# Layer norms at the end of a projection: last two output tiles by token halves, the root's guess in PSUM, and the second half's sums inside the next stage's loop

## What is computed

```python
for layer in range(2):
    if layer == 0: mix = concat(s5_mixer(...), stick_breaking(...)) @ w_out_ab
    else:          mix = hgrn2_mixer(...) @ w_out_c
    h = layer_norm(ALPHA * h + mix, ln_mix_g[layer], ln_mix_b[layer])
    hid = square(relu(h @ mlp_w_up[layer] + mlp_b_up[layer]))
    h = layer_norm(ALPHA * h + hid @ mlp_w_down[layer] + mlp_b_down[layer], ln_mlp_g[layer], ln_mlp_b[layer])
return h[:, N_META:, :]
```

## Time and profile before

| | |
|---|---|
| median of 3 runs | 1380.58 us (1379.8 to 1380.92) |
| the profiled execution | 1380.39 us, its span 1378.5 us |
| granted TensorE clock, mean | 0.987 |
| PE busy | 1323.0 us, 96% of the span |
| DVE, ACT, POOL busy | 45%, 37%, 38% |
| chain that ended last, by engine | PE 83%, DVE 6%, ACT 6% |

### The profile page before, as it was taken

How to read it: one execution, slowest core, us unless ns; L and a number is a source line. 1 busy time by engine, 2 the same in 40 slices (tenths; PEclk the granted TensorE clock), 3 DMA queues, 4 the chain that set the end, 5 groups by cost and what they waited for, 6 DMA issues and landing times.

```text
span 1378.5 us, 21807 instructions
## 1 busy us (share of the span) xinstructions
PE 1323.0 (96%) x9502; PEld 1185.7 (86%) x9502; DVE 624.2 (45%) x1048; ACT 512.8 (37%) x734; POOL 530.4 (38%) x224
## 2 busy tenths in 40 slices
PE   6999998999999999999999999998999999999996
PEld 5998855999999999999998988876798888888885
DVE  6899544456530024412456456464556300344125
ACT  4334487435222222221365335263362222223124
POOL 1001153355443344454554123145654444444450
PEclk9999999999999999999999999999999999999998
DMA  6211200121333322333211111112212333323321
GB/s 181 92 62 33 63 1 0 62 92 62 93 92 92 93 92 92 92 93 92 92 62 62 62 62 62 61 63 91 92 62 92 92 94 107 105 92 92 92 62 61
DMA packets 141791, 108.27 MB, mean 79 GB/s; under 512 B 8096, under 2 KB 139376, under 8 KB 141696
## 3 DMA queue, kind: packets, MB, share of 16 engines
q1 hardware_dynamic: 141296, 106.77, 25.6%
q10 hardware_dynamic: 400, 0.11, 0.0%
HBM read 104.77 MB, written 2.10 MB: 78 GB/s over the span
## 4 chain that ended last, share of the span: by engine, by line
PE 83%; DVE 6%; ACT 6%; issue 2%; POOL 1%; DMA 1%; DVEq 0%; SPq 0%; ACTq 0%
PE pb L709 62%; PE pb L875 2%; PE pb L721 2%; PE pb L876 2%; PE pb L877 2%; PE pb L1076 1%; PE pb L815 1%; PE pb L816 1%; ACT wh L1292 1%; PE pb L753 1%; PE pb L814 1%; PE pb L1074 1%; DVE bc L2276 1%; DVE st L2315 1%; PE pb L985 1%
## 5 line engine op out<-in xcount | busy, mean ns | idle before, releaser
L565 POOL TENSOR_TENSOR wl<-raw,wh 128x2048 fp32r<-128x2048 f32 x85 | 396.6, 4666 | 531.1 <-ACT wh L1292 531.1
L709 PE MATMUL pb<-hh,wh 128*128 128x264 f32 (+1 forms) x1160 | 302.0, 318 | 1.8 <-DVE tmp L2098 1.2
L709 PE MATMUL pb<-hh,wl 128*128 128x264 f32 (+1 forms) x1160 | 297.5, 314 | 0.0
L709 PE MATMUL pb<-hl,wh 128*128 128x264 f32 (+1 forms) x1160 | 297.3, 314 | 0.0
L1292 ACT ACTIVATE wh<-raw 128x2048 fp32r<-128x2048 f32 x97 | 185.0, 1908 | 96.7 <-DMA raw<-in_mlp_w_down 63.2
L709 PEld LDWEIGHTS pb<-hh,wh 128*128 128x128 f32 x1160 | 191.2, 189 | 17.6 <-issue 3.7
L709 PEld LDWEIGHTS pb<-hl,wh 128*128 128x128 f32 x1160 | 191.2, 189 | 13.9 <-issue 1.2
L709 PEld LDWEIGHTS pb<-hh,wl 128*128 128x128 f32 x1160 | 191.1, 189 | 13.5
L709 PE MATMUL pb<-hidh,wh 128*128 128x264 f32 (+1 forms) x720 | 191.9, 321 | 0.0
L709 PE MATMUL pb<-hidh,wl 128*128 128x264 f32 (+1 forms) x720 | 191.1, 320 | 0.0
L709 PE MATMUL pb<-hidl,wh 128*128 128x264 f32 (+1 forms) x720 | 190.3, 318 | 0.0
(11 more groups left out here) (391 smaller groups left out, 2055.3 us busy)
## 6 DMA issues: line engine op xcount, KB each, us to landing
raw<-in_mlp_w_up SPq DMA_DIRECT2D x32, 1024.0 KB, 5.3
raw<-in_mlp_w_down SPq DMA_DIRECT2D x32, 1024.0 KB, 5.5
raw<-in_w_in_c SPq DMA_DIRECT2D x16, 1024.0 KB, 5.3
raw<-in_w_in_ab SPq DMA_DIRECT2D x8, 1024.0 KB, 5.6
raw<-in_w_out_ab SPq DMA_DIRECT2D x4, 1024.0 KB, 5.0
raw<-in_w_out_c SPq DMA_DIRECT2D x4, 1024.0 KB, 4.9
x_tok<-in_x SPq DMA_DIRECT2D x2, 1024.0 KB, 8.0
raw<-in_s_w_glu SPq DMA_DIRECT2D x1, 1024.0 KB, 5.4
```

Source lines behind the costliest of these rows:

```text
L565: pool.tensor_tensor(wl[:, c % RING, :], raw[:, c % RING, :], wh[:, c % RING, :].bitcast(F32), ALU.subtract).then_inc(w_lo, 1)
L709: mm = pe.matmul(pb[:, bank + b, 0:z_ - a], lhs, rhs[:, a:z_], start=first and hi and k == 0, stop=last and k == len(todo) - 1)
```

## The change

`TWO` is true for norms 0 and 2. The counts that semaphores are compared with get helper tables (`DS`, `SQ`, `SC`, `CT` in place of `n`, `6 * n`, `9 * n`, `13 * n`), since norms 0 and 2 now count one more each.

1. Norms 0 and 2: tiles 6 and 7 both run by token halves, in the order tile 6 a = 0, tile 7 a = 0, tile 6 a = 1, tile 7 a = 1. The four sums of the first half go into the products of tile 6 a = 1. DVE's addition of tile 6, its total, ACT's square and POOL's addition of that square become two halves each. The second ones follow later: on DVE after the first `scale_`, on ACT ahead of `last_square(1)`, on POOL after the first `hl`.
2. All norms: the second half's `first_sum` and `first_squares` leave the end of the stage. They are issued in `run_after` after step 1's and step 3's hh products; `last_square(1)` goes from step 2 to step 3. In norm 3 they go between the transposes of blocks 0 and 1.
3. All norms: ACT writes its guess into PSUM (`ln_part(name, 4, a)`), and DVE's three operations are rewritten so that each reads at most `total` or `tmq` from SBUF beside it.

```diff
+TWO = (True, False, True, False)
+DS = [n + sum(TWO[:n]) for n in range(4)]
...
@@ POOL, lows_ln @@
+                def add_half(a):
+                    pool.wait_ge(squared, SC[n] + (9 if a else 7))
+                    pool.wait_ge(sq_added, SQ[n] + 5)
+                    s_ = part(name, sqs[:, :], a)
+                    pool.tensor_tensor(s_, s_, part(name, squares(6), a), ALU.add).then_inc(sq_added, 1)
...
-                    if t >= 4:
+                    if t == 6 and TWO[n]:
+                        add_half(0)
+                    elif t >= 4:
                         add(t)
...
+                            if a == 0 and m == 0 and TWO[n]:
+                                add_half(1)
@@ PE, last_tile @@
-                first_sum(name, n, 1)
-                first_squares(name, n, 1)
+            def last_tiles(name, n, rh, rl, c, w0, order):
+                kcs = len(order)
+                for a in range(2):
+                    for t in (6, 7):
+                        if a == 0 and t == 7:
+                            pe.wait_ge(*free_bank(name, 7))
+                        for i, kc in enumerate(order):
+                            mm = products_half(name, t, c, w0(kc, t), rh[:, kc, :], rl[:, kc, :], a, i == 0, i == kcs - 1)
+                            if i == kcs - 1:
+                                mm.then_inc(tile_done if a else half_done, 1)
+                            if a and t == 6 and i == 2:
+                                first_sum(name, n, 0)
+                                last_sum(name, n, 0)
+                            if a and t == 6 and i == 4:
+                                first_squares(name, n, 0)
+                            if a and t == 6 and i == 6:
+                                last_square(name, n, 0)
@@ PE, run_after @@
-                pe.wait_ge(*free_bank(tiles[0][0], 0))
+                if not TWO[n]:
+                    pe.wait_ge(*free_bank(tiles[0][0], 0))
...
                         if a == 0 and step == 1:
+                            first_sum(LN_STAGE[n], n, 1)
                             last_sum(LN_STAGE[n], n, 1)
-                        if a == 0 and step == 2:
+                        if a == 0 and step == 3:
+                            first_squares(LN_STAGE[n], n, 1)
                             last_square(LN_STAGE[n], n, 1)
@@ PE, transposes behind norm 3 @@
                     if a == 0 and kc == 0:
+                        first_sum("down11", 3, 1)
                         last_sum("down11", 3, 1)
                     if a == 0 and kc == 1:
+                        first_squares("down11", 3, 1)
                         last_square("down11", 3, 1)
@@ ACT, run_ln @@
                 def guess(a):
-                    guess_inv_sqrt(part(name, total[:, :], a), part(name, tmq[:, 0, :], a), var_out, 2 * n + 1 + a)
+                    act.wait_ge(var_out, 2 * n + 1 + a)
+                    o = part(name, tmq[:, 0, :], a)
+                    me.step(act.activation(o, part(name, total[:, :], a), ACT.Ln))
+                    me.settle()
+                    act.activation(ln_part(name, 4, a), o, ACT.Exp, scale=-0.5).then_inc(guessed, 1)
...
                         if a == 0 and m == 1:
+                            if TWO[n]:
+                                square_half(1)
                             last_square(1)
@@ DVE, layer_norm @@
-                add(6)
-                TT(tot, tops, hm(6), ALU.add).then_inc(d_summed, 1)
+                if TWO[n]:
+                    add_half(0)
+                    dve.wait_ge(centred, CT[n] + 11)
+                    me.settle()
+                    total_half(0)
+                else:
+                    add(6)
+                    TT(tot, tops, hm(6), ALU.add).then_inc(d_summed, 1)
...
                 def root(a):
-                    inv_sqrt(part(name, tmq[:, 0, :], a), part(name, total[:, :], a), part(name, tmq[:, 1, :], a),
-                             ln_part(name, 4, a), 2 * n + 1 + a + (8 if n >= 2 else 0))
+                    o, t = ln_part(name, 4, a), part(name, tmq[:, 1, :], a)
+                    dve.wait_ge(guessed, 2 * n + 1 + a + (8 if n >= 2 else 0))
+                    step(TT(t, part(name, total[:, :], a), o, ALU.mult))
+                    step(STT(t, t, -0.5, o, ALU.mult, ALU.mult))
+                    step(STT(o, t, 1.5, o, ALU.add, ALU.mult))
...
                     scale_(m, 0)
+                    if m == 0 and TWO[n]:
+                        add_half(1)
                     if m == 0:
                         last_add(1)
+                    if m == 0 and TWO[n]:
+                        total_half(1)
```

More of the change, by code:

```diff
@@ L64 @@
          2: [("up10", 0), ("up10", 1), ("up10", 2), ("up10", 3)]}
+TWO = (True, False, True, False)
+DS = [n + sum(TWO[:n]) for n in range(4)]
+SQ = [6 * n + sum(TWO[:n]) for n in range(4)]
+SC = [9 * n + sum(TWO[:n]) for n in range(4)]
+CT = [13 * n + sum(TWO[:n]) for n in range(4)]
 AHEAD = {"up00": 2, "f0": 1, "q0": 1, "up10": 2}
@@ L735, in run @@
                             pe.wait_ge(*free_bank(name, t))
+                        if norm is not None and TWO[norm] and t == KC - 2:
+                            last_tiles(name, norm, rh, rl, s0 + j, lambda kc, t: kc * cols_ + (t % 2) * P, order or range(kcs))
+                            return
                         if norm is not None and t == KC - 1:
@@ L1580, in square, with square_half @@
                 def square(m):
-                    act.wait_ge(centred, 13 * n + (m + 1 if m < 4 else m + 5))
+                    act.wait_ge(centred, CT[n] + (m + 1 if m < 4 else m + 5))
                     if m >= 2:
-                        act.wait_ge(sq_added, 6 * n + m - 2)
+                        act.wait_ge(sq_added, SQ[n] + m - 2)
                     act.activation(flat(name, squares(m)), flat(name, h[:, m, :]), ACT.Square).then_inc(squared, 1)
+                def square_half(a):
+                    act.wait_ge(centred, CT[n] + (13 if a else 11))
+                    act.wait_ge(sq_added, SQ[n] + 4)
+                    act.activation(part(name, squares(6), a), part(name, h[:, 6, :], a), ACT.Square).then_inc(squared, 1)
                 def last_square(a):
-                    act.wait_ge(centred, 13 * n + 12 + a)
-                    act.wait_ge(sq_added, 6 * n + 5)
+                    act.wait_ge(centred, CT[n] + 12 + (a + TWO[n] if a else 0))
+                    act.wait_ge(sq_added, SQ[n] + 5)
                     act.activation(part(name, tmq[:, 1, :], a), part(name, h[:, 7, :], a), ACT.Square).then_inc(squared, 1)
@@ L1601, in run_ln @@
                             square(m)
-                    if t >= 4:
+                    if t == 6 and TWO[n]:
+                        square_half(0)
+                    elif t >= 4:
                         square(t)
@@ L2166, in layer_norm, with add_half, total_half @@
                 step(TT(tops, tops, hm(5), ALU.add))
-                add(6)
-                TT(tot, tops, hm(6), ALU.add).then_inc(d_summed, 1)
+                def add_half(a):
+                    if a:
+                        dve.wait_ge(tile_done, t0 + 7)
+                    else:
+                        dve.wait_ge(half_done, DS[n] + 1)
+                    h6 = part(name, h[:, 6, :], a)
+                    TT(h6, h6, pb[:, a, 0:width(name)], ALU.add).then_inc(centred, 1)
+                def total_half(a):
+                    TT(part(name, total[:, :], a), ln_part(name, 6, a), part(name, h[:, 6, :], a),
+                       ALU.add).then_inc(d_summed, 1)
                 def last_add(a):
-                    dve.wait_ge(tile_done if a else half_done, t0 + KC if a else n + 1)
+                    if a:
+                        dve.wait_ge(tile_done, t0 + KC)
+                    else:
+                        dve.wait_ge(half_done, DS[n] + 1 + TWO[n])
                     h7 = part(name, h[:, 7, :], a)
@@ L2198, in layer_norm @@
                 last_add(0)
-                dve.wait_ge(squared, 9 * n + 7)
+                dve.wait_ge(squared, SC[n] + 7)
                 dve.wait_ge(s1_squared, 2 * n + 1)
```

25 lines of the change are left out of this document (13 added, 12 removed).

## The result

After took 1380.19 us (median of 20 runs, 1376.32 to 1384.24); before, run beside it, 1375.14 us (median of 20, 1374.17 to 1380.92). The ratio of the two is **1.0027, 95% interval 1.0016 to 1.0038**: after is slower, by 3.7 us (2.2 to 5.2). The ratio is that of the means (1380.42 and 1376.65); the medians lie 5.1 us apart, because that of before falls into the shorter of its two groups of executions. The forecast was 1382.6 us and +2.0 us. Two things in the forecast caused this: the level that it started from, and the clock at norm 0.

The account below looks back on a forecast made before the run. Each seam was taken to hang on the second half's last square; its shifts of +0.13, +1.46, +0.40 and 0 us at norms 0 to 3 made +2.0, giving 1382.6 us against the median, range 1380.4 to 1385.0.

Parts of the forecast that it names:

- What bounds the seam: From one product stage to the next, the first pass's last `hl` group trails the second half's last square by 9.4-9.6 us.
- Q: The second half's last square at each norm; the time from the old stage's end to it sets the cost there.
- 1, the earlier start: Norms 0 and 2: token halves bring the first half's variance 1.45 and 0.88 us sooner, partly held by POOL's copy.
- 2, the root: DVE's first root step takes 0.42 us, saving 0.19, 1.92 and 0.83 us in norms 0, 1 and 2.
- 3, from the first scaling to Q: Norms 0 and 2: this path takes 8.63 us, where it was 6.86 and 6.52; called the term that decides.
- Norm 1: Tiles kept; step 1 starts 0.87 us sooner, but the second half's last square comes at 688.40, 1.46 us later.
- Norm 3: Last square moves by one sum, from 1360.23 to about 1360.67; effect on the time 0 (0 to 0.1).
- The sum: Last square after less before: norm 0 +0.13, norm 1 +1.46, norm 2 +0.40, norm 3 0; together +2.0 us.
- the first rival: PE's clock falls again behind norm 0, 2 or both, or before lost it less often: +1.4 to +3.4 us; chance 0.30.
- The base: Time of before that the forecast started from: profiled execution 1380.39 us, 0.19 below the median of the runs.
- The rival for faster: The second pass follows the first `hh`, so each earlier start counts: 4.2 us less, 1376.4; chance 0.07.
- The third rival: DVE's root goes on waiting for POOL's copy: 1.9 us more, 1384.5; chance 0.06.

Follow-up runs that it names:

- run 6: Before with part 3 of the change alone (guess in PSUM), plus `high` moved from behind block 5 to block 7 and POOL's quarter copies later: 1365.01 us, ratio 0.9926.
- run 7: After with `high` moved from behind block 5 to behind block 7 and POOL's quarter copies moved later: 1371.4 us, ratio 0.9975.
- run 11: After with the second half's squares back at step 2, and `high` and POOL's quarter copies moved later: 1370.1 us, ratio 0.9951.
- run 5: After with the second half's first_squares and last_square back from step 3 to step 2: 1376.43 us, ratio 1.0002.
- run 2: Before with part 3 of the change alone (guess in PSUM, DVE's three operations rewritten): 1372.53 us, ratio 0.9972.
- run 4: After with the old root (guess in SBUF, guess * guess first): one execution, 1384.9 us.
- run 10: After with small useless products in both of PE's waits in norms 0 and 2 (4 ahead of step 0, 5 behind it): 1378.57 us, ratio 1.001.
- run 9: After, unchanged, run once more for more executions and a second trace: 1379.36 us, ratio 1.0022.
- run 8: Before with small useless products (8 at norm 0, 11 at norm 2) in PE's wait for the first `hh`: 1371.33 us, ratio 0.9977.

## Why the prediction was right or wrong, point by point

- **What bounds the seam**: right. The last hl group followed Q by 9.4 to 9.6 us in every kernel that kept the queue, and by 7 to 8.1 us where `high` was moved (runs 6, 7, 11). One step less before Q was one step less of seam, three times (run 5).
- **1, the earlier start**: right. From the addition of tile 5, the first half's variance was forecast at 10.55 and 10.45 us and came at 10.65 and 10.53; the wait for POOL's copy is there, smaller (0.18 us in norm 0, and 0.42 in norm 2 for 0.8).
- **2, the root**: the step is 0.43 at once, as forecast. The Trainium skill, "SBUF — State Buffer", section "Who interferes with whom", says that a VectorE instruction with at most one SBUF input, outside its two-port modes, doesn't contend with GpSimd, and that one with two SBUF inputs contends with a GpSimd instruction that reads SBUF; the traces agree (0.43 us beside POOL's copy in after and run 2; 1.42 with two such inputs in run 4). The root's price in norm 0 of after was too low, as run 4 shows (1.0 for 0.19 us), but that changed nothing in the sum, which was worked out for the two parts together: the first scaling was forecast 13.40 and 13.27 us after the addition, and came at 13.48 and 13.31.
- **3, from the first scaling to Q**: 8.63 forecast; 8.37 in norm 2 (21.68 - 13.31), 8.5 in norm 0 at full clock (run 10). The waits ahead of and behind step 0 are 0.85 and 0.8 us, not 1.2 each; the sum of the path was right.
- **Norm 1**: Q at 32.22 forecast (688.40 less 656.18), 32.22 measured; the seam +1.46, as forecast. **Norm 3**: Q 0.41 later, end the same.
- **The sum**: +0.13, +1.46, +0.40, 0 forecast; +1.6, +1.5, +0.15, 0.0 measured against the second trace of before. **The step that failed in it is the clock at norm 0.** I took it that two short waits would keep it. It fell again in both traces of after, and that costs 1.6 us (45.68 against the 44.05 of run 10), which is the first rival, at the one seam; at norm 2 it held. The rival had 0.30. Why it falls at one seam and not at the other stays open: run 7 held it at norm 0 behind waits of 0.85 and 0.80 us. The Trainium skill, "TensorE: Matmul & The Clock Gate", section "HAM oscillation — how this bites in real kernels", warns of long idle gaps; by it the clock would have held at both. The trace of norm 0 (a fall behind 0.85 and 0.82 us) speaks against it, that of norm 2 (none behind 0.88 and 0.80) for it. The next section of that page of the Trainium skill, "A second HAM failure mode: psum-queue depth-cycling", tells of a bf16 kernel in which frequent short idle times between groups of products make the clock fall. Norm 0 is nearer to that, norm 2 isn't, and the forecast did not weigh it.
- **The base**: the other step that failed. 1380.58 us was taken as the time of before; it is that of executions with a slow clock in the attention part, and the batch has its median at 1375.14, 5.4 us lower. I had seen stretches with the clock at half outside the seams and did not ask whether they belong to every execution. The range took in less clock at the seams of before, not less elsewhere. By the forecast's +2.0 on 1375.14 the time would have been 1377.1, by the measured ratio it is 1378.9, and the median of after, which falls between its short and its long executions, is 1380.19. That the miss of the range is so small is luck: the base was 5.4 us too high and the rise of the median 3.1 too low (5.1 for 2.0), and the two cancel in part. From the right base, the same range would have run from 1375.0 to 1379.6, with the time above it. How much of the medians' 5.1 us is chance, by which executions had the slow stretch, isn't settled; the seams account for 3.3.
- **The rival for faster** did not come, though the first scaling did come sooner at each of the three seams. **The third rival** (the root goes on waiting) is ruled out by its own row.
- Right in sign and on the path at each seam; wrong in size by one fall of the clock, and in level by one reading. No run tried what else the clock might hang on.

## What to carry to other kernels

Look for the event that the end of a stage hangs on, by finding what keeps a fixed distance to it at several seams; starting the other end of the pipeline sooner gave only what it moved that event by, and moving one 1.9 us copy (with the quarter copies that follow it) out of the chain behind that event, at three seams, gave 6 to 8 us (runs 6, 7 and 11 against 2, 9 and 5), falls of the clock that went away included. An operation that reads two operands from SBUF beside a long copy on POOL is worth rewriting so that one of them lies in PSUM: here it took 0.43 us for 0.61 to 2.34. Before a time is taken as the base of a forecast, compare the clock in its trace stretch by stretch with a second execution.

## What the runs showed of the hardware that was not expected

- The granted clock falls at different places in executions of one kernel. Before had 168.6 us as one such place in its first trace and not in its second, and most executions lie in two groups some 5 us apart.
- At norm 0 the clock fell after two waits of 0.85 and 0.82 us with step 0 between them; at norm 2 it held through 0.88 and 0.80 (both traces of after), and in run 2 through one of 1.78 us at norm 0. The same two waits at norm 0 (0.85 and 0.80 us) held it in run 7 and lost it in run 11; one wait of 1.79 us at norm 2 held it in run 6 and lost it in run 2. So the length of the wait alone does not tell; what else decides was not settled.
- Some 0.22 us products without use, put into PE's waits, paid for themselves in run 8 (ratio 0.9977); in run 10 a gain is not clear of noise.
